# Softmax scores computed keys by queries instead of queries by keys, in a fused attention layer

## The chip, the cores and the metric

One core of one Trainium2 chip runs the whole layer. The metric is device time in microseconds (us) of one execution, the median over runs. Engines are named as the profile names them: PE is TensorE (PEld its weight loads), DVE VectorE, ACT ScalarE, POOL GpSimd, SP the engine that issues most DMAs.

## The reference, cut to what matters

A layer over 1024 tokens of width 1024: an input projection, a gated linear attention group (GLA, 4 heads, 16 chunks of 64), a softmax attention group (MLA, 8 heads, key width 96, value width 64), an output projection with residual, and a squared-ReLU MLP. The change touches the softmax attention:

```python
def one_block(args):                      # a block of 128 queries
    q_blk, blk = args
    s = jnp.einsum('bhqd,bhkd->bhqk', q_blk, kh, preferred_element_type=jnp.float32) * scale
    q_chunk = (blk * QBLOCK + jnp.arange(QBLOCK)) // CHUNK
    mask = key_chunk[None, :] <= q_chunk[:, None]         # CHUNK = 64
    p = jax.nn.softmax(jnp.where(mask, s, -1e30), axis=-1)
    return jnp.einsum('bhqk,bhkv->bhqv', p.astype(vh.dtype), vh)
```

Everything is float32. The projections and the MLP split each operand into a rounded part (type `fp32r`, names ending in `_hi`) and a remainder (`_lo`) and add three products. The softmax attention and the GLA products run in plain f32.

## The kernel before, in words

The program is written engine by engine; each engine walks its own fixed list of instructions, and semaphores tie the lists together. Stages follow each other: input projection (32 tiles, `in_project`, with the preparation of queries, keys and values behind it), attention, output projection (16 tiles, `project`), MLP up and MLP down.

The attention loop has 64 steps, one for each head and block of 128 queries (`STEPS`), two heads interleaved; 16 steps make a pair of heads, and there are four pairs. One step is this chain:

- PE `scores` (called two steps ahead): queries are the weights, keys are streamed, the result is 128 queries by up to 1024 keys in PSUM (banks 0 to 3).
- DVE `row_max` (L1627, L1630) writes the mask value into the corner that the block may not see and takes the negated maximum of each row.
- ACT `exp` (L1167) computes the exponential with that maximum as bias and adds up the row.
- DVE `row_sum` (L1634) takes the reciprocal of the sum, one column; POOL `normalize` (L907) multiplies the row by it.
- PE `p_transposes` (L2163) turns each 128x128 block, because the value product needs keys on the partitions; ACT and DVE `pT_copy` (L975, L1641) copy them out of PSUM banks 4 and 5.
- PE `values`: for two heads at once, each in its own 64 columns of the array, values are the weights and the turned exponentials are streamed, into bank 6.
- ACT `mla_mix_hi` and DVE `mla_mix_lo` split a finished unit (two heads by 512 queries) for the output projection.

Between these, every engine runs its share of GLA (`gla(c, n)`: chunk pair c in eight small stages n, all in PSUM bank 7). Stage 7 makes the output, ACT squares it (L1158), DVE sums the squares (L1587), POOL forms the reciprocal root (L796, L797), DVE scales the output (`og`, L1346), PE transposes it (L2083). In the loop before, stages 0 to 7 fall on consecutive steps.

The first two `scores` stand ahead of the last input projection tile (tile 31). The last transposes and values run inside the first two output projection tiles. PE's waits in `scores` are on ACT's exponentials two tiles back; SP loads queries, keys and GLA chunks one unit ahead (L570, L577, L584) and starts the pieces of the output weights (L549) at the start of the loop.

Of the kernel before, what the change touches and what calls it, by code (L numbers as in the profile page):

```python
# [12 lines left out]
P = 128  # L13
# [73 lines left out]
def layer(nc, x, positions, attn_norm, w_in, w_gate_up, b_gate, gla_out_norm, q_a_norm, w_uq,  # L87
# [9 lines left out]
    with ctx:  # L97
# [9 lines left out]
        def at(name, shape, offset, dt=F32):  # L107
# [56 lines left out]
        m_pT = at("m_pT", [P, 3, NB, P], 72 * KB)  # L164

        m_p = [at(f"m_p{n}", [P, T], offset * KB) for n, offset in enumerate((68, 88, 64))]
        m_v = at("m_v", [P, NB, MH * MV], 128 * KB)

        m_qT = [at(f"m_qT{n}", [DQK, 2, W], (144 + 4 * n) * KB) for n in range(2)]
        m_kT = [[at(f"m_kT{n}_{s}", [DQK, T], offset * KB) for s, offset in enumerate(places)]  # L170
                for n, places in enumerate(((152, 156), (84, 92)))]

        ke_tok = at("ke_tok", [P, GH * GDK], 168 * KB)
# [76 lines left out]
        m_nm = small("m_nm", [P, 2])  # L250
        m_sum = small("m_sum", [P, NB])
        m_rden = small("m_rden", [P, NB])
# [51 lines left out]
        q_in, k_in, z_in, v_in = ([sem(f"{name}{n}") for n in range(2)] for name in ("q_in", "k_in", "z_in", "v_in"))  # L304
        s_ready, max_ready, p_ready, rden_ready = sem("s_ready"), sem("max_ready"), sem("p_ready"), sem("rden_ready")
        pn_ready = sem("pn_ready")
        pT_ready, pT_out, pT_out2, pv_done = sem("pT_ready"), sem("pT_out"), sem("pT_out2"), sem("pv_done")
# [28 lines left out]

        def own_place(q, k):
            return q == 0 and k >= RING
# [16 lines left out]
        def low_by_vector(n):  # L355


            return KT <= n < KT * IN_GROUPS and n % KT in (2, 3, 4, 5)
# [142 lines left out]
        ORDER = (0, 3, 1, 2), (4, 7, 5, 6)  # L501
        STEPS = [(2 * p + s, b) for p in range(MH // 2) for half in range(2) for b in ORDER[half] for s in range(2)]
        UNIT = NB

        BEHIND = 3

        def half_of(i):
            return i // UNIT % 2

        def score_banks(i):  # L510

            return ((3, 2, 0, 1)[i % 4],) if half_of(i) == 0 else (2 * (i % 2), 2 * (i % 2) + 1)

        def scores_at(i):
            first, n = score_banks(i)[0], len(score_banks(i))
            return ps[:, first:first + n, :].rearrange("p a n -> p (a n)")

        def before_in_banks(i):

            return max((n for n in range(i) if set(score_banks(n)) & set(score_banks(i))), default=None)  # L520


        def by_scalar(i):
            return half_of(i) == 1 or i % 2 == 0

        def by_vector(i):
            return half_of(i) == 1 or i % 2 == 1

        def scalar_copies(i):

            return sum(by_scalar(n) for n in range(i + 1))

        def vector_copies(i):
            return sum(by_vector(n) for n in range(i + 1))

        def mix_due(i):

            j = (i - BEHIND) // 2
            if i >= BEHIND and (i - BEHIND) % 2 == 0 and j % 4 == 3:
                return j // 8, j // 4 % 2  # L540
            return None

        @block.sync
        def _(sp):
# [20 lines left out]
            def queries(u):  # L565

                if u >= 2:
                    sp.wait_ge(s_ready, UNIT * (u - 1))
                p, half = divmod(u, 2)
                sp.dma_start(m_qT[u % 2][:, :, :], q_d[2 * p:2 * p + 2, :, half * W:(half + 1) * W].rearrange("h d t -> d h t")  # L570
                             ).then_inc(q_in[u % 2], 16)

            def keys(p):
                if p >= 2:
                    sp.wait_ge(s_ready, 2 * UNIT * (p - 1))
                for s in range(2):
                    sp.dma_start(m_kT[p % 2][s][:, :], k_d[2 * p + s]).then_inc(k_in[p % 2], 16)  # L577
# [9 lines left out]
            def stores(s):  # L587
# [18 lines left out]
                if s == HEADS_T_AT[-1]:  # L606
                    sp.wait_ge(heads_stored, 32 * NB)
                    sp.wait_ge(v_stored, 16 * NB)
                    queries(0)
                    keys(0)  # L610
                    for n in range(2):
                        half = slice(n * NB // 2, (n + 1) * NB // 2)
                        sp.dma_start(m_v[:, half, :], v_d[half].rearrange("b p n -> p b n")).then_inc(v_in[n], 16)
                    queries(1)

            for q in range(IN_GROUPS):
# [10 lines left out]
                if q + 1 < IN_GROUPS:  # L627
                    for k in range(RING + 2, KT):
                        in_piece(q + 1, k)
                    if q == 0:  # L630
                        sp.dma_start(m_ukv[:, :], w_ukv[0]).then_inc(mla_w_in, 16)
                else:
                    for k in range(RING):
                        piece(IN_GROUPS, k, w_out_d[0, row_tile(IN_GROUPS, k)])
# [3 lines left out]
            for n in range(2):  # L638
                sp.wait_ge(z_stored[n], 16 * NB)
            for c in range(2):  # L640
                chunk_in(c)

            sp.wait_ge(z_ready, NB * IN_GROUPS)
            keys(1)
            for u in range(2, MH):
                if u % 2 == 0 and u >= 4:
                    keys(u // 2)
                queries(u)
                chunk_in(u)
# [3 lines left out]
            sp.wait_ge(pv_done, len(STEPS) // 2)  # L653
# [131 lines left out]
        def _(pool):  # L785
# [116 lines left out]
            def normalize(i):  # L902

                _, b = STEPS[i]
                rows = m_p[i % 3][:, 0:(b + 1) * P]
                pool.wait_ge(rden_ready, i + 1)
                pool.tensor_scalar(rows, rows, m_rden[:, i % NB:i % NB + 1], 1.0, ALU.mult, ALU.mult).then_inc(pn_ready, 1)  # L907

            for i in range(len(STEPS)):
                c, n = divmod(i, NB)  # L910
                normalize(i)
                if i == 0:
                    decays(0)
# [4 lines left out]
                if c == NB - 1 and n >= 1:  # L918
                    low_part(IN_GROUPS, n - 1)
            low_part(IN_GROUPS, KT - 1)  # L920
# [44 lines left out]
        def _(act):  # L965
# [194 lines left out]
            def exp(i):  # L1160
                h, b = STEPS[i]
                nk = (b + 1) * P
                act.wait_ge(max_ready, i + 1)
                if i >= 3:

                    act.wait_ge(pT_ready, 2 * (i - 2))
                act.activation(m_p[i % 3][:, 0:nk], scores_at(i)[:, 0:nk], ACT.Exp, bias=m_nm[:, i % 2:i % 2 + 1],  # L1167
                               accum_out=m_sum[:, i % NB:i % NB + 1]).then_inc(p_ready, 1)

            def pT_copy(i):  # L1170
                if by_scalar(i):
                    _, b = STEPS[i]
                    act.wait_ge(pT_ready, 2 * i + 1 + (half_of(i) == 0))
                    bank, n = (4, 4) if half_of(i) else (4 + i % 2, b + 1)
                    copy(m_pT[:, i % 3, 0:n, :], bank4(bank)[:, 0:n, :]).then_inc(pT_out, 1)
# [1153 lines left out]
```

## Time and profile before

| | us |
|---|---|
| median of 3 runs (1137.91 to 1140.94) | 1139.54 |
| the profiled execution: its own time | 1140.02 |
| the profiled execution: span from the first to the last instruction | 1138.0 |
| TensorE clock granted, mean over the span | 0.997 of full |

The page gives busy time per engine, then the chain of work that ended last, then groups of instructions. An engine that is busy 98% of the span is not at its peak, because the ends of pipelined matmuls are modelled: the distance between the starts of two matmuls says what one really takes. A plain f32 matmul leaves two records (two passes over its columns), an `fp32r` matmul and a transpose one. The attention stage runs from 237.4 us to 433.9 us of the span.

### The profile page before, as it was taken

What the parts mean: (1) busy time and instruction counts of PE and PEld (TensorE: products, weight loads), DVE (VectorE), ACT (ScalarE), POOL (GpSimd) and SP (SyncE); (2) the same over time, 40 slices, a digit from 0 to 9 for tenths busy, and PEclk for the clock granted to TensorE, in tenths of its full rate; (3) what the DMA queues carried; (4) which work ended last, traced back from release to release, by engine and by line L of the source; (5) the groups of instructions that cost most, each with busy time, mean ns of one, the idle gap of its engine ahead of it and who ended that gap; (6) DMA issues with size and microseconds to landing.
All of it is one profiled execution on the core that took longest, in us unless ns stands there. A gap on an engine that the chain in (4) does not pass through costs nothing.

```text
span 1138.0 us, 15337 instructions
## 1 busy us (share of the span) xinstructions
PE 1117.6 (98%) x5630; PEld 908.8 (80%) x5630; DVE 778.1 (68%) x1120; ACT 463.9 (41%) x876; POOL 511.2 (45%) x418
## 2 busy tenths in 40 slices
PE   7999999999999999999999999999999999999998
PEld 7978888776676678887888888888878888888887
DVE  5565767557777652278485875587797978888863
ACT  5343554336555552156223322332334334434341
POOL 2332513114433463147654444444545556565562
PEclk9999999999999999999999999999999999999999
DMA  7232523461221016213544333431789783457542
GB/s 253 67 130 74 167 84 112 116 194 33 61 74 47 26 38 240 74 75 111 161 137 142 116 112 130 139 121 37 261 277 359 234 290 121 139 180 232 197 119 86
DMA packets 98554, 158.41 MB, mean 139 GB/s; under 512 B 9329, under 2 KB 39041, under 8 KB 98481
## 3 DMA queue, kind: packets, MB, share of 16 engines
q1 hardware_dynamic: 96864, 152.80, 40.6%
q10 hardware_dynamic: 1296, 4.46, 1.1%
q8 instruction: 45, 0.74, 0.3%
q0 software_dynamic: 320, 0.19, 0.2%
q14 instruction: 29, 0.23, 0.1%
HBM read 115.47 MB, written 41.94 MB: 138 GB/s over the span
## 4 chain that ended last, share of the span: by engine, by line
PE 85%; DVE 7%; POOL 2%; ACT 2%; issue 2%; DMA 2%; SPq 0%; ACTq 0%; DVEq 0%; POOLq 0%
PE ps L1919 80%; PE ps L2163 2%; PE ps L2012 1%; DVE t_all L1691 1%; POOL tx_lo L932 1%; DVE dr_lo L1691 1%; DVE m_nm L1630 1%; DMA up_raw<-in_w_up_dram 1%; DMA raw<-in_w_in_dram 1%; PE ps L1934 1%; DMA m_ukv<-in_w_ukv_dram 1%; POOL ua_lo L937 1%; DVE state L1346 0%; DVE stage L1691 0%; POOL a_lo L932 0%
## 5 line engine op out<-in xcount | busy, mean ns | idle before, releaser
L1919 PE MATMUL ps<-dr_hi,dl_hi 128*128 128x512 f32 x448 | 175.1, 391 | 1.6 <-DVE dr_lo L1691 1.6
L1919 PE MATMUL ps<-dr_hi,dl_lo 128*128 128x512 f32 x448 | 175.0, 391 | 0.0
L1919 PE MATMUL ps<-dr_lo,dl_hi 128*128 128x512 f32 x448 | 174.9, 390 | 0.0
L937 POOL TENSOR_TENSOR ua_lo<-up_raw,ua_hi 128x1024 fp32r<-128x1024 f32 x46 | 116.7, 2541 | 117.0 <-ACT ua_hi L975 117.0
L961 POOL TENSOR_TENSOR dl_lo<-l_raw,dl_hi 128x512 fp32r<-128x512 f32 x64 | 100.3, 1593 | 72.7 <-ACT dl_hi L975 72.3
L961 POOL TENSOR_TENSOR dl_lo<-s_all,dl_hi 128x512 fp32r<-128x512 f32 x48 | 75.3, 1589 | 58.4 <-ACT dl_hi L975 57.6
L1919 PEld LDWEIGHTS ps<-dr_hi,dl_hi 128*128 128x128 f32 x448 | 84.5, 189 | 20.3 <-issue 2.8
L1919 PE MATMUL ps<-a_hi,ua_hi 128*128 128x512 f32 x256 | 99.9, 390 | 0.6 <-POOL ua_lo L937 0.6
L1919 PE MATMUL ps<-a_hi,ua_lo 128*128 128x512 f32 x256 | 99.6, 389 | 0.0
L1919 PE MATMUL ps<-a_lo,ua_hi 128*128 128x512 f32 x256 | 99.6, 389 | 0.0
L1919 PEld LDWEIGHTS ps<-dr_hi,dl_lo 128*128 128x128 f32 x448 | 84.4, 188 | 17.7
L1919 PEld LDWEIGHTS ps<-dr_lo,dl_hi 128*128 128x128 f32 x448 | 84.5, 189 | 17.4
L907 POOL TENSOR_SCALAR m_p<-m_p,m_rden 128x128 f32<-128x128 f32 (+7 forms) x64 | 52.9, 829 | 96.7 <-DVE m_rden L1634 96.2
L975 ACT ACTIVATE ua_hi<-up_raw 128x1024 fp32r<-128x1024 f32 x48 | 50.5, 1057 | 90.6 <-PE ps L1919 79.0
L1691 DVE TENSOR_TENSOR dr_lo<-r_raw,dr_hi 128x512 fp32r<-128x512 f32 x64 | 72.2, 1127 | 13.2 <-ACT dr_hi L975 13.1
L1919 PE MATMUL ps<-wi_hi,a_hi 128*128 128x512 f32 (+1 forms) x192 | 75.4, 393 | 2.8 <-DVE a_lo L1357 2.7
L1919 PE MATMUL ps<-m_kT,m_qT 96*128 96x512 f32 (+3 forms) x192 | 75.8, 505 | 1.2 <-ACT m_p L1167 1.2
L1691 DVE TENSOR_TENSOR dr_lo<-t_all,dr_hi 128x512 fp32r<-128x512 f32 x48 | 59.9, 1263 | 22.7 <-ACT dr_hi L975 22.3
L1919 PE MATMUL ps<-tx_hi,ua_hi 128*128 128x512 f32 x192 | 74.7, 389 | 0.0
L1919 PE MATMUL ps<-tx_lo,ua_hi 128*128 128x512 f32 x192 | 74.7, 389 | 0.0
L1919 PE MATMUL ps<-tx_hi,ua_lo 128*128 128x512 f32 x192 | 74.7, 389 | 0.0
L975 ACT ACTIVATE dl_hi<-l_raw 128x512 fp32r<-128x512 f32 x64 | 39.8, 622 | 85.1 <-PE ps L1919 79.3
(238 smaller groups left out, 2536.4 us busy)
## 6 DMA issues: line engine op xcount, KB each, us to landing
r_raw<-in_w_down_dram SPq DMA_DIRECT2D x144, 256.0 KB, 3.5
hidden<-stage SPq DMA_DIRECT2D x72, 256.0 KB, 2.0
up_raw<-in_w_up_dram SPq DMA_DIRECT2D x16, 1024.0 KB, 5.5
l_raw<-hidden SPq DMA_DIRECT2D x64, 256.0 KB, 3.6
raw<-in_w_in_dram SPq DMA_DIRECT2D x24, 256.0 KB, 3.5
z_gla<-z_stage SPq DMA_DIRECT2D x16, 256.0 KB, 2.0
raw<-in_w_out_dram SPq DMA_DIRECT2D x16, 256.0 KB, 6.4
xs<-in_x_dram SPq DMA_DIRECT2D x8, 512.0 KB, 7.6
```

The costliest lines, as they stand in the source:

```text
L907: pool.tensor_scalar(rows, rows, m_rden[:, i % NB:i % NB + 1], 1.0, ALU.mult, ALU.mult).then_inc(pn_ready, 1)
L932: pool.tensor_tensor(lo, t_new[n][:, :, :], hi.bitcast(F32), ALU.subtract).then_inc(tlo_done, 1)
L937: pool.tensor_tensor(ua_lo[n % UP_RING][:, :, :], up_source(g, product), ua_hi[n % UP_RING][:, :, :].bitcast(F32), ALU.subtract).then_inc( ...
L961: pool.tensor_tensor(slot(dl_lo, t), left_source(t), slot(dl_hi, t).bitcast(F32), ALU.subtract).then_inc(dllo_done, 1)
L975: return act.activation(dst, src, ACT.Copy, scale=scale)
L1630: dve.tensor_reduce(m_nm[:, i % 2:i % 2 + 1], s[:, 0:nk], AX.X, ALU.max, negate=True).then_inc(max_ready, 1)
L1691: return dve.tensor_tensor(out_, in0, in1, op)
L1919: return pe.matmul(dst, lhsT, rhs, start=start, stop=stop, skip_group_check=onto)
L1934: last = pe.transpose(bank4(4 + j)[:, i, :], src[:, (4 * j + i) * P:(4 * j + i + 1) * P], ident[:, :])
L2012: last = pe.transpose(bank4(4 + i // 4, DQK)[:, i % 4, :], m_qk[:, b % 2, i, :], ident[:, :])
L2163: last = pe.transpose(bank4(bank)[:, c % 4, :], m_p[i % 3][:, c * P:(c + 1) * P], ident[:, :])
```

## The change

It replaces the attention loop. Scores are computed with keys as the weights and queries streamed, so the exponentials come out with keys on the partitions, which is what the value product takes. The row maximum must then be known before the scores: a first pass (`estimate`) computes queries by keys from operands rounded to `fp32r`, DVE takes the maxima of that, PE turns the table of maxima once for a unit, and a DMA lays it as row 97 of the queries; a row of ones stands under the keys, so the score product subtracts the maximum itself. Sums over keys now run across partitions: POOL adds up the exponential tiles of a unit, and PE multiplies that by a matrix of ones (`sums`, bank 4). DVE then takes the reciprocal of 512 columns and multiplies the finished unit (`mla_divide`).

The loop has 24 steps of two tiles (a tile: 128 keys by up to 512 queries, two heads), six steps (S0, S1, L0 to L3) for a pair of heads: S steps belong to the first 512 queries (4 tiles), L steps to the second 512 (8 tiles). Each pair takes 12 estimates, 12 tiles, 2 turns, 2 sums. The places of GLA stages are given by a table. Input projection tiles 29 to 31 are interleaved with the first nine estimates. The first pieces of the output weights are loaded when the last pair begins.

```diff
+        STEPS = 6 * MH // 2
+        TILES = [(u, c) for u in range(UNITS) for c in range(NB // 2 * (u % 2 + 1))]
+        ESTIMATES = {(S0, 0): (1, 5), (S0, 1): (1, 6), (S0, 2): (1, 7), (L0, 2): (2, 0), (L0, 3): (2, 1), (L1, 1): (2, 2),
+                     (L1, 2): (2, 3), (L2, 0): (3, 0), (L2, 1): (3, 1), (L2, 2): (3, 2), (L2, 3): (3, 3), (L3, 1): (3, 4)}
+        GLA_AT = ((-1, 0, 1, 2), (None, 3, None, None), (4, None, 5, 6), (7, 8, 9, 10), (11, 12, None, 13),
+                  (None, 14, None, None))
...
+            def maxima(u):
+                sp.wait_ge(turned_out, u + 1)
+                sp.dma_start(m_q[queries_at(u)][DQK:DQK + 1, :, :].rearrange("o s (b n) -> o (s b) n", n=P),
+                             m_row[:, u % 2, :]).then_inc(q_in[u % 3], 16)
...
-            def normalize(i):
...
-                pool.tensor_scalar(rows, rows, m_rden[:, i % NB:i % NB + 1], 1.0, ALU.mult, ALU.mult).then_inc(pn_ready, 1)
...
+            def add(j):
...
+                pool.tensor_tensor(total, total, p_tile(j)[:, :, seen], ALU.add).then_inc(sum_done, 1)
...
+            def round_queries(u):
...
+                copy(m_q_hi[n][:, :, :], m_q[n][0:DQK, :, :]).then_inc(mla_hi, 1)
+            def round_keys(p):
...
+                copy(m_k_hi[keys_hi_at(p)][:, :, :], m_k[p % 2][0:DQK, :, :]).then_inc(mla_hi, 1)
...
+            def exp(j):
...
+                to, scores = p_tile(j), ps[:, score_bank(j):score_bank(j) + 2, :]
+                first = first_query(j)
+                if diagonal(j):
+                    own = slice(first, first + CHUNK)
+                    act.activation(to[CHUNK:P, :, own], ident[CHUNK:P, :].rearrange("p (s n) -> p s n", s=2), ACT.Copy, scale=0.0)
+                    act.activation(to[0:CHUNK, :, own], scores[0:CHUNK, :, own], ACT.Exp)
+                    first += CHUNK
+                act.activation(to[:, :, first:W], scores[:, :, first:W], ACT.Exp).then_inc(p_ready, 1)
...
+            def mla_divide(u):
+                dve.wait_ge(den_ready, u + 1)
+                dve.wait_ge(raw_out, u + 1)
+                step(dve.reciprocal(ps[:, 4, :], ps[:, 4, :]))
+                dve.tensor_tensor(m_raw[u][:, :], m_raw[u][:, :], ps[:, 4, :], ALU.mult).then_inc(raw_ready, 1)
...
+            def estimate(e):
...
+                    pe.wait_ge(max_ready, e)
+                if sums_before(e):
+                    pe.wait_ge(raw_ready, sums_before(e))
...
+            def sums(u, estimates):
+                pe.wait_ge(max_ready, estimates)
+                if u >= 1:
+                    pe.wait_ge(raw_ready, u)
+                pe.wait_ge(sum_done, in_ring(first_of(u + 1)))
+                for s in range(2):
+                    last = mm(ps[s * MV:(s + 1) * MV, 4, :], ones[:, 0:MV], p_first[u % 2][:, s, :], True, True)
...
+            def scores(j):
...
+                for s in range(2):
+                    last = mm(ps[:, score_bank(j) + s, seen], m_k[p % 2][:, s, c * P:(c + 1) * P],
+                              m_q[queries_at(u)][:, s, seen], True, True)
...
+            for d in range(STEPS):
+                between_scores(d, 0)
+                if d >= 1:
+                    scores(2 * d)
+                linear(d, 0)
+                between_scores(d, 1)
+                scores(2 * d + 1)
+                linear(d, 1)
+                between_scores(d, 2)
+                if d >= 1:
+                    values(d - 1)
+                linear(d, 2)
+                between_scores(d, 3)
+                linear(d, 3)
+                between_scores(d, 4)
```

## Rows read from the trace of the kernel before

**Rows 1.** The page: busy time of the engines, and the chain by engine.
```profile
PE 1117.6 (98%) x5630; PEld 908.8 (80%) x5630; DVE 778.1 (68%) x1120; ACT 463.9 (41%) x876; POOL 511.2 (45%) x418
...
PE 85%; DVE 7%; POOL 2%; ACT 2%; issue 2%; DMA 2%; SPq 0%; ACTq 0%; DVEq 0%; POOLq 0%
```

**Rows 2.** One pair's stretch: length, busy PE, PEld, DVE, ACT, POOL, clock, DMA.
```profile
291.40:336.80 45.40, 43.85 (x334) 31.30 (x333) 33.01 (x94) 25.56 (x63) 18.61 (x24) 1.00 0.20 59
```

**Rows 3.** Timeline: start, length; f32 scores, transposes, values, `fp32r` products.
```profile
297.33 0.38 PE L2163 MATMUL ps<-ident,m_p 128*128 128x128 f32 x2
...
297.64 1.09 PE L1919 MATMUL ps<-m_pT,m_v 128*64 128x128 f32 x16
...
299.64 0.19 PEld L1919 LDWEIGHTS ps<-m_kT,m_qT 96*128 96x128 f32 x1 [0.24 <-issue]
300.07 0.19 PEld L1919 LDWEIGHTS ps<-m_kT,m_qT 96*128 96x128 f32 x1 [0.24 <-issue]
...
314.24 1.06 PE L2163 MATMUL ps<-ident,m_p 128*128 128x128 f32 x8
...
315.24 1.31 PE L1919 MATMUL ps<-m_pT,m_v 128*64 128x128 f32 x20
...
422.05 0.39 PE L1919 MATMUL ps<-w_hi,a_hi 128*128 128x512 f32 x1
...
424.76 0.39 PE L1919 MATMUL ps<-w_hi,a_hi 128*128 128x512 f32 x1
```

**Rows 4.** Groups of 291.4 to 336.8 us: PE, with count, busy us, mean ns, idle.
```profile
L1919 PE MATMUL ps<-m_kT,m_qT 96*128 96x512 f32 x24 | 12.5, 614 | 0.3 <-ACT m_p L1167 0.3
L2163 PE MATMUL ps<-ident,m_p 128*128 128x128 f32 x73 | 10.9, 274 | 0.7 <-DVE m_pT L1641 0.7
```

**Rows 5.** The same stretch, DVE: reductions, GLA work, reciprocal, two-input product.
```profile
L1346 DVE SCALAR_TENSOR_TENSOR state<-state,decay,ps 64x128 f32<-64x128 f32 x8 | 2.8, 346 | 0.9 <-PE ps L1919 0.8
L1634 DVE RECIPROCAL m_rden<-m_sum 128x1 f32<-128x1 f32 x16 | 2.5, 156 | 1.2 <-ACT m_p L1167 1.2
L1630 DVE TENSOR_REDUCE m_nm<-ps 128x1 f32<-128x1024 f32 x2 | 2.4, 1224 | 0.1
L1346 DVE SCALAR_TENSOR_TENSOR og<-ps,g_rs,zg 128x128 f32<-128x128 f32 x8 | 2.2, 338 | 0.0
L1587 DVE TENSOR_REDUCE g_ss<-osq 128x4 f32<-128x512 f32 x2 | 1.4, 676 | 1.0 <-ACT osq L1158 1.0
L1555 DVE TENSOR_TENSOR g_ks<-g_ks,zqkT 128x256 f32<-128x256 f32 x2 | 0.8, 410 | 0.0
```

**Rows 6.** The page and the stretch of rows 4: POOL and ACT.
```profile
L937 POOL TENSOR_TENSOR ua_lo<-up_raw,ua_hi 128x1024 fp32r<-128x1024 f32 x46 | 116.7, 2541 | 117.0 <-ACT ua_hi L975 117.0
L975 ACT ACTIVATE ua_hi<-up_raw 128x1024 fp32r<-128x1024 f32 x48 | 50.5, 1057 | 90.6 <-PE ps L1919 79.0
L797 POOL TENSOR_TENSOR g_rs<-g_rs,minus_half 128x4 f32<-128x4 f32 x2 | 2.0, 1014 | 0.2
L1167 ACT ACTIVATE m_p<-ps,m_nm 128x1024 f32<-128x1024 f32 x2 | 2.2, 1114 | 1.9 <-DVE m_nm L1630 1.9
```

**Rows 7.** DVE elsewhere: a product of 512 columns (52 to 66 us), a scan.
```profile
L1503 DVE TENSOR_TENSOR wi_lo<-raw,wi_hi 128x512 fp32r<-128x512 f32 x4 | 2.5, 685 | 0.0
...
L1446 DVE TENSOR_TENSOR_SCAN g_cum<-ones,g_cum 128x128 f32<-128x128 f32 x16 | 5.3, 401 | 0.1
```

**Rows 8.** Timeline at the start of attention: key loads and DVE's scan.
```profile
221.39 1.00 SPq L577 DMA_DIRECT2D m_kT<-k_heads  x2
...
228.32 2.63 DVE L1446 TENSOR_TENSOR_SCAN g_cum<-ones,g_cum 128x128 f32<-128x128 f32 x8
```

**Rows 9.** Key tiles, 214 to 240 us: from issue to landing.
```profile
DMA to landing us min/median/max: 5.4/5.7/5.9
```

**Rows 10.** Timeline at the end of attention: first projection product, last values.
```profile
421.27 0.48 PE L1919 MATMUL ps<-w_hi,a_hi 128*128 128x512 f32 x1
...
431.79 1.75 PE L1919 MATMUL ps<-m_pT,m_v 128*64 128x128 f32 x28
```

More of the change, by code:

```diff
@@ L495, in layer @@
         GATE_T, SOFTPLUS, GATE_SUMS = NB, 3 * NB, 3 * NB + 3
[L501 to L540, printed above, removed]
-            return None
+        UNITS = MH
@@ L1655, in _ @@
+            for s in range(NB * IN_GROUPS - 4, NB * IN_GROUPS - 1):
+                tile_out(s)
+                behind(s)
+                if s == NB * IN_GROUPS - 3:
+                    for e in (2, 3, 4):
+                        row_max(e)
+                    gla_decays(0)
+                elif s < NB * IN_GROUPS - 3:
+                    for e in (0, 1):
+                        row_max(e)
+            for e in (5, 6):
+                row_max(e)
             gla_decayed(0)
+            for e in (7, 8):
+                row_max(e)
@@ L1954, in in_project @@
                 for k in range(KT):
-                    if between is not None and k == KT - 2:
-                        between()
+                    if k in between:
+                        between[k]()
                     if n in LOGIT_TILES and k == 3:
@@ new lines, in values @@
+            def values(d):
+                for j in (2 * d, 2 * d + 1):
+                    u, c = TILES[j]
+                    pe.wait_ge(p_ready, j + 1)
+                    if j == 0:
+                        pe.wait_ge(v_in, 16 * MH // 2)
+                    if c == 0 and u >= 1:
+                        pe.wait_ge(raw_out, u)
+                    seen = slice(first_query(j), W)
+                    for s in range(2):
+                        last = mm(ps[s * MV:(s + 1) * MV, 6, seen], m_v[:, u // 2, c, s * MV:(s + 1) * MV],
+                                  p_tile(j)[:, s, seen], c == 0, j + 1 == first_of(u + 1), True)
+                    last.then_inc(pv_done, 1)
@@ new lines, in between_scores, with linear @@
+            def between_scores(d, place):
+                if estimate_at(d, place) is not None:
+                    estimate(estimate_at(d, place))
+                if turned_at(d, place) is not None:
+                    turn(turned_at(d, place))
+                u = sums_at(d, place)
+                if u is not None:
+                    sums(u, min(first_of(u + 2) + 2 if u % 2 == 0 else first_of(u + 3), len(TILES)))
+            def linear(d, place):
+                if gla_at(d, place):
+                    gla(*gla_at(d, place))
@@ new lines, in _ @@
+            for n in range(NB * IN_GROUPS - 3, NB * IN_GROUPS):
+                in_project(*divmod(n, NB), {
+                    NB * IN_GROUPS - 3: {4: lambda: estimate(0), 6: lambda: estimate(1)},
+                    NB * IN_GROUPS - 2: {0: lambda: estimate(2), 2: lambda: estimate(3), 4: lambda: turn(0), 6: lambda: estimate(4)},
+                    NB * IN_GROUPS - 1: {0: lambda: estimate(5), 2: lambda: estimate(6), 3: lambda: scores(0),
+                                         4: lambda: estimate(7), 6: lambda: estimate(8)}}[n])
```

520 lines of the change are left out of this document (313 added, 207 removed).

## The prediction

> **What bounds the kernel now.** The page comes first. PE is busy 98% of the span and carries 85% of the chain that ended last, so the time is the sum of what PE issues and of what it waits for; other engines count only where PE stands behind them [rows 1]. The stretches show the attention loop repeating with a period of 45.4 us, one pair of heads each (four in all, three of them alike), at a granted clock of 1.00, the upper level (2.4 GHz). DVE is busy for 33.0 us of a period, ACT for 25.6, POOL for 18.6 [rows 2]. The timeline gives what a matmul really takes. Two passes of an f32 score start 0.43 us apart for 512 columns. Eight transposes last 1.06 us with a tail of 0.27, so one takes (1.06 - 0.27)/7 = 0.113. Twenty value records take (1.31 - 0.27)/19 = 0.055 each for 128 columns, half of what scores take per column, because two heads run side by side. Twelve `fp32r` products of 512 columns take 2.71, 0.226 each. A change of group costs about 0.1: two transposes (0.23) are followed by values after 0.31 [rows 3].
>
> Work of a period: scores 9216 columns, 15.4 us; 72 transposes, 8.1; values 7.9; GLA, whose 68 records go by the same rates, 7.1. Sum 38.5. What is left to 45.4, 6.9 us, is some 50 changes of group (5) and waits; the groups name 1.0 of these, on the copies of turned exponentials (0.7) and on ACT (0.3) [rows 4].
>
> **The change, part by part, for one pair of heads.**
>
> Transposes go: -8.1 us. Scores and values keep their columns: 0. The copies of turned exponentials and POOL's normalization were hidden under PE save for the waits named above; they are worth no more than those.
>
> Estimates come: 12 of them, 9472 columns at 0.226 for 512: +4.2. Sums: two units of four passes of 512 columns. If the two halves run side by side as values do, a unit costs 2 x 0.43 = 0.86, if not 1.72 [rows 3]; I take 1.1, nearer the row of values, as the form is the same: +2.2. Two turns: +0.2. PE's work becomes 37.0, 1.5 less. Changes of group: 12 scores, 12 estimates, 12 tiles of values of which half need a wait of their own, 2 turns, 2 sums, 12 of GLA, about 45, 4.5 us. PE alone would need 41.5 against 45.4.
>
> The new waits decide. I walked one period, engine by engine, in the order of the lists.
>
> S0: PE issues estimate, scores, the GLA output, estimate, scores, estimate, short values, and stands before the transposes of `og` after 7.3 us. The output ended at 4.1. Behind it DVE takes a row maximum (1.22, with the mask's corner 1.4), the sum of squares (0.68), POOL the root (1.01 and a short one), DVE a second row maximum in its shadow and `og` (four of 0.34 that overlap, 1.1): 9.3 [rows 5, 6]. Wait: 1.9. Before, these stages lay on consecutive steps of 2.8 us, now on places some 1.5 us apart.
>
> Behind the transposes in PE's list stand the turn and the next step's scores, so ACT's exponentials start later by as much. L0: `sums` wait for the row maximum of the second estimate, which on DVE is queued behind the GLA state (four of 0.35): 1.5. L1: `og` again, 1.4. S1, L2 and L3 show none above 0.2. Together 4.8, and a period of 41.5 + 4.8 = 46.3, 0.9 more than before.
>
> The division. DVE takes a reciprocal of 512 columns twice a pair, where it took 16 of one column. No row shows a wide one. The lower bound is one column per step like the two-input product, 0.14 + 512 x 1.07 ns = 0.69. DVE's scan takes (401 - 135)/128 = 2.1 ns per column [rows 7], so operations do differ; this would give 1.2. The one-column reciprocal takes 156 ns where the line through the products of 256 columns (410) and of 512 (685) leaves 136 for one column [rows 5, 7]: 20 ns for a single column, which read as the price of a column would be 10 us for 512, the upper bound. Part of these 20 may be start-up. I take eight steps per column, 8 x 512 x 1.07 ns + 0.14 = 4.5 us, between the two and nearer the row of the same instruction.
>
> The Trainium skill (page VectorE: DVE Perf Modes, section First, the fixed hardware budget) says that reciprocal runs on iterative divide operations "with a repeat count of 8". With the rate of an ordinary pass the sum would be the first rival's below, with eight steps it is mine.
>
> At 4.5 us the division is 3.8 longer than an ordinary pass. In L0 and L1: the sums end at 24.0 in the period, the division at 29.2; PE comes to the estimate that needs bank 4 free at 27.5, and waits 1.7. In S1 the odd unit's division ends 3.8 later; ACT's list has the split of that unit (which needs it) ahead of rounding queries (1.06) and keys (2 x 1.06) and of the next exponential [rows 6]; the copy of a GLA tile behind these comes 1.0 late for PE. Together 2.7 per pair; the first pair has no odd unit before it and the last no estimates after it: 1.6 + 2.7 + 2.7 + 1.0 = 8.0.
>
> Hidden, and what if not: exponentials, 28 instructions a pair instead of 16 with no sum read out, some 15 us of 46 on ACT (1024 columns 1.11) [rows 6]; if late, `scores` wait two tiles on. POOL's adds, 7168 columns a pair at 2.54 for 1024: 17.8 [rows 6], in place of the normalizations; behind a ring of four tiles; if late, `sums` come first. The DMA of the maxima: turned at the end of S0, needed a step later, about 2.5 us against 4.8. On SP's list it stands behind loads of keys, queries and chunks, and these wait only for things done earlier.
>
> **Start.** Keys are issued at 221.4 and land 5.7 later, at 227.1 [rows 8, 9]; ACT rounds keys (2.1) and queries (1.06): 230.2. The first estimate stands at 229.3 in tile 29: 0.9 of waiting. DVE is held by its scan until 231.0 [rows 8], which delays the second one little. The nine estimates and the first scores are work that the loop has less of. The turns wait for row maxima of 1.22: 1.6. Start: +2.5. The first pair has no `og` in S0: -1.9.
>
> **End.** Before, projection starts at 421.27, with the last transposes and values (1.75) left inside its first two tiles [rows 10]. After, only sums and `og` are left. The output weights are loaded later, and their fourth to seventh piece hang on remainders made in the last two steps; I count 0 for it, and up to 3 if a piece is late.
>
> **Sum** against the profiled execution's own 1140.0 (span 1138.0 and 2.0 around it): 4 x 0.9 - 1.9 + 2.5 + 8.0 = +12.2; the last pair also drops 1.5 of waits of L0, where no estimates stand: +10.7. That is 1150.7, and 0.5 less on the scale of the median 1139.5: 1150. A difference under 0.3%, 3.4 us, can't be told from none.
>
> **Rivals.**
>
> First: the wide reciprocal runs like any pass. Then the 8.0 go: 1142, within 0.3%. For it: nearly all DVE rows lie on one line. Against: the 20 ns. It takes the place of the forecast if the group of wide reciprocals shows under 1.5. Range 1138 to 1147. Chance 0.2.
>
> Second, the faster end: PE stays the bound, because the chains on DVE are shorter than I walked them. DVE loses 12 copies of 3840 columns (3840 x 1.07 ns + 12 x 0.14 = 5.8 a period) and the small reciprocals (2.5) and gains 2 x 1.4; its load falls from 33 to some 27.5 of 45 [rows 2, 5]. If every wait above is covered, a pair takes 41.5, and 4 x 3.9 = 15.6 are saved, less 2.5 at the start: 1127. With half of the waits left, 1136. It decides from the point where `og` reaches PE within 3.2 us of the GLA output. Against: that chain has 1.37 + 0.68 + 1.2 + 1.1 us in it. Chance 0.25.
>
> Third: DVE becomes the bound. With 4.5 for a division, DVE has 27 + 7.6 = 35 us of work in 46; if a division near the upper bound (10 us) is true, every step falls behind and a pair takes about 6 us more than in my forecast: 1170. Chance 0.08.
>
> Fourth: the change doesn't remove what it says, for instance values of 512 columns no longer run side by side. Then values cost 7.9 more a pair: 1180. Against: the rows of values and of the GLA form both overlap in narrow columns. Chance 0.02.
>
> My forecast keeps 0.45, with a range of its own of 1144 to 1158.
>
> **How the numbers follow.** Faster by over 0.3% (under 1136): the second rival, 0.25. Within: most of the first and the edge of the forecast, 0.17. Slower: 0.58. The range leaves out the third and fourth rival above and the lower half of the second below: 1130 to 1161.
>
> **What would show each step.** In the changed profile: the group of RECIPROCAL 128x512 at 4.5 us, not 0.7; PE idle before the transposes of `og` released by DVE, 1.4 to 1.9 us, seven times; PE idle before estimates released by DVE's product into `m_raw`; busy time by period 46 to 49 us instead of 45.4. Wrong it would be if the period is under 44 us, if PE's idle time sits on ACT or POOL instead of DVE, or if the first scores of a unit wait for the DMA of the maxima.

## The result, and the profile after

The changed kernel takes 1198.86 us (median of 4 runs, 1198.18 to 1199.98), the kernel before 1138.93 beside it: a ratio of 1.0525, 95% interval 1.0507 to 1.0543. That is 60 us slower. The forecast was 1150, 11 us slower, with a range that ended at 1161: right in sign, wrong in size by more than the range allowed. All ratios here are of undisturbed executions; one of the kernel before, 1323 us at a mean clock of 0.794, is left out beside the fifth plan.

The page of the changed kernel: its span, busy times, the slices of PE and of the granted clock, and the chain by engine.

```profile
span 1198.2 us, 14071 instructions
...
PE 1151.5 (96%) x5094; PEld 891.6 (74%) x5094; DVE 796.5 (66%) x996; ACT 466.8 (39%) x842; POOL 523.7 (44%) x390
...
PE   8999999987979798999999999999999999999998
...
PEclk9999999987878787999999999999999999999999
...
PE 84%; DVE 9%; issue 2%; POOL 2%; DMA 2%; ACT 1%; SPq 0%; DVEq 0%; ACTq 0%; POOLq 0%
```

PE's busy time went up from 1117.6 to 1151.5 us though it issues 536 matmuls fewer [rows 1]. Work of fewer columns that takes longer is the sign of a lower clock, and the row PEclk shows it: 8 and 7 in the attention (slices 9 to 16), and nowhere else. Now the same in stretches; the columns are those of [rows 2], the clock third from the end.

```profile
319.30:380.70 61.40, 52.63 (x200) 27.43 (x200) 37.25 (x62) 24.82 (x54) 22.93 (x18) 0.81 0.16 43
...
244.00:480.00 236.00, 203.69 (x750) 105.78 (x750) 136.68 (x225) 95.93 (x202) 90.60 (x70) 0.80 0.14 40
```

A pair of heads takes 61.4 us; it took 45.4 [rows 2]. From the first scores to the first product of the output projection the attention takes 240.1 us (244.1 to 484.2) in place of 183.6, so 56.5 us of the loss are in it; the first scores stand 6.4 later, and some 3 come back behind. The clock in the attention stood at 1.00 before and at 0.80 now. Inside a pair it has two levels:

```profile
283.00:287.00 4.00, 0.86 (x5) 0.43 (x5) 3.23 (x5) 0.29 (x2) 3.86 (x2) 1.00 0.00 0
287.00:304.00 17.00, 15.34 (x33) 7.46 (x34) 4.52 (x9) 4.44 (x9) 6.90 (x4) 0.50 0.10 32
304.00:317.00 13.00, 11.97 (x62) 7.23 (x61) 10.39 (x20) 6.97 (x19) 3.23 (x5) 0.99 0.38 91
```

For 4 us (283 to 287) PE is busy for 0.86. Then comes a stretch of 17 us in which PE is busy 90% of the time and the granted clock is 0.50, the lower of its two levels (1.2 GHz); PE does 33 matmuls in it, against 62 in the next 13 us. This repeats in each of the first three pairs; in the fourth the clock stays at 0.50 for some 14 us. What does PE wait for? The waits of PE in the pair from 319.3 us (in total, times, longest):

```profile
PE ps L2281 <- DVE og L1523: 4.8, 2, 3.1
PE ps L2114 <- DVE m_nm L1804: 2.0, 1, 2.0
PE ps L2114 <- ACT m_q_hi L1083: 1.7, 1, 1.7
PE ps L2114 <- DVE m_nm L1809: 0.2, 1, 0.2
```

Together 8.7 us, of which four waits make 8.5: 1.7 before `og`'s transposes in S0, 2.0 before the sums at the end of L0, 3.1 before `og`'s transposes in L1 and, right behind these, 1.7 before the first estimate of L2. The timeline of L1 shows how the two come together (DVE, then PE, then POOL, then ACT):

```profile
340.75 0.96 DVE L1804 TENSOR_REDUCE m_nm<-ps 128x2 f32<-128x768 f32 x1
341.62 0.68 DVE L1764 TENSOR_REDUCE g_ss<-osq 128x4 f32<-128x512 f32 x1
342.73 0.17 DVE L1803 MEMSET ps<- 64x128 f32 x1 [0.43 <-PE ps L2114]
342.93 1.23 DVE L1804 TENSOR_REDUCE m_nm<-ps 128x2 f32<-128x1024 f32 x1
344.07 2.62 DVE L1819 TENSOR_TENSOR a_lo<-m_raw,a_hi 128x512 fp32r<-128x512 f32 x1
346.62 1.11 DVE L1523 SCALAR_TENSOR_TENSOR og<-ps,g_rs,zg 128x128 f32<-128x128 f32 x4
```

```profile
344.44 0.27 PE L2354 MATMUL ps<-ident,m_nm 128*8 128x128 f32 x1
347.79 0.66 PE L2281 MATMUL ps<-ident,og 128*128 128x128 f32 x4 [3.08 <-DVE og L1523]
350.16 0.87 PE L2114 MATMUL ps<-m_k_hi,m_q_hi 96*128 96x320 f32 x2 [1.72 <-ACT m_q_hi L1083]
```

```profile
343.80 7.59 POOL L1009 TENSOR_TENSOR p_first<-p_first,p_ring 128x1024 f32<-128x1024 f32 x3
```

```profile
348.48 0.60 ACT L1083 ACTIVATE a_hi<-ps 128x512 fp32r<-128x512 f32 x1 [3.46 <-PE ps L2281]
348.97 1.04 ACT L1083 ACTIVATE m_q_hi<-m_q 96x1024 fp32r<-96x1024 f32 x1
```

DVE's list has `mla_mix_lo` (L1819) ahead of `og`. A product of 512 columns took 0.685 us before [rows 7]; this one takes 2.62, while POOL adds. `og` ends at 347.7, PE transposes, and ACT, whose list has the copy of the transposed tile ahead of the rounding of the queries, gives PE its next estimate only at 350.0. So it goes in the first three pairs. In the fourth no adds stand beside the lower part, which takes 0.68 us (at 462.0), and `og` waits for POOL's root instead; PE waits the same 3.1.

And the division, the largest unknown of the forecast, with the lower part of the MLA tile (groups of DVE, 240 to 430 us):

```profile
L1814 DVE RECIPROCAL ps<-ps 128x512 f32<-128x512 f32 x5 | 16.8, 3367 | 2.8 <-PE ps L2114 2.8
L1819 DVE TENSOR_TENSOR a_lo<-m_raw,a_hi 128x512 fp32r<-128x512 f32 x5 | 9.7, 1936 | 0.7 <-ACT a_hi L1083 0.7
```

3.37 us, where I had taken 4.5. So the clock, the waits and the division stand beside each other as possible causes. The theory (A): the waits make up some 9 us a pair, and what is more, they make the clock fall, which costs as much again. The rivals: (B) the new mixture of products lowers the clock, whatever the waits; (C) the clock is a bystander and the waits are the loss; (D) the division holds up the chains.

### The profile page after: what moved, and what is told of

Same layout as the page of the kernel before. It is cut to its first block, busy times and chain, and to the rows that moved or that the text cites. A ratio compares the mean times of both kernels' runs of the same rounds, so it can differ in the third digit from the quotient of the medians.

```text
span 1198.2 us, 14071 instructions
## 1 busy us (share of the span) xinstructions
PE 1151.5 (96%) x5094; PEld 891.6 (74%) x5094; DVE 796.5 (66%) x996; ACT 466.8 (39%) x842; POOL 523.7 (44%) x390
## 4 chain that ended last, share of the span: by engine, by line
PE 84%; DVE 9%; issue 2%; POOL 2%; DMA 2%; ACT 1%; SPq 0%; DVEq 0%; ACTq 0%; POOLq 0%
PE ps L2114 81%; PE ps L2210 1%; DVE t_all L1886 1%; POOL tx_lo L1040 1%; DVE m_nm L1809 1%; DVE a_lo L1819 1%; DVE dr_lo L1886 1%; DVE og L1523 1%; DMA up_raw<-in_w_up_dram 1%; PE ps L2281 1%; DMA raw<-in_w_in_dram 1%; PE ps L2129 1%; POOL ua_lo L1045 0%; DMA m_ukv<-in_w_ukv_dram 0%; DVE stage L1886 0%
## 5 line engine op out<-in xcount | busy, mean ns | idle before, releaser
L2114 PEld LDWEIGHTS ps<-dr_hi,dl_lo 128*128 128x128 f32 x448 | 84.1, 188 | 17.4
L1009 POOL TENSOR_TENSOR p_first<-p_first,p_ring 128x1024 f32<-128x1024 f32 (+3 forms) x40 | 69.9, 1747 | 60.3 <-PE ps L2114 35.0
L2114 PE MATMUL ps<-m_q,m_k 97*128 97x512 f32 (+3 forms) x192 | 89.4, 600 | 0.0
L2114 PE MATMUL ps<-wi_hi,a_lo 128*128 128x512 f32 (+1 forms) x192 | 73.5, 383 | 0.0
```

The lines of the kernel that those rows point to most:

```text
L1009: pool.tensor_tensor(total, total, p_tile(j)[:, :, seen], ALU.add).then_inc(sum_done, 1)
L2114: return pe.matmul(dst, lhsT, rhs, start=start, stop=stop, skip_group_check=onto)
```

## The experiments

**Filling the waits.** Products whose results nobody reads, in front of the four waits (the lines that call `fill` are left out; in the diffs that follow, too, only the lines that carry the change are shown):

```diff
+ def fill(d, n):
+     pe.wait_ge(p_ready, 2 * d + 1)
+     for i in range(n):
+         mm(ps[:, 2, 0:P], ident[:, :], ident[:, :], True, True)
+ FILL = {(S0, 3, "gla"): 8, (L1, 3, "gla"): 13, (L2, 0, "est"): 8, (L0, 4, "est"): 9}
```

> Adds matrix products of the identity with itself (128 columns, f32, about 0.23 us each at the full clock, results never read) on TensorE ahead of the four waits: 8 before the output transposes in the first step of a pair, 9 before the sums in the third, 13 before the output transposes in the fourth, 8 before the estimate that opens the fifth; they fill about 9 us of each pair's 61.4. Theory A (the clock falls because TensorE stands idle in these waits, and that is most of the loss): the granted clock of the attention is back at 1.00, the pair takes 51 to 53 us, the kernel 1155 to 1168 us. Rival B (the clock falls because of the new mixture of products, whatever the waits): the clock stays near 0.80, the time 1198 or more. Rival C (the waits themselves are the loss and the clock a bystander): 1198.

Measured: 1169.98 us, ratio 1.0272 (1.0254 to 1.0289), 29 us faster than the changed kernel, with nothing taken from it and 152 products added. A pair of it:

```profile
326.40:378.40 52.00, 50.89 (x274) 31.93 (x274) 37.15 (x63) 24.84 (x53) 22.96 (x18) 1.00 0.19 52
```

52.0 us at a clock of 1.00. B falls, since all of the new mixture is in it; C falls, since PE can start its useful work no sooner than before: the products that fill the four places take 9.2 us of the pair, the waits there took 8.5. DVE, ACT and POOL do the same work in the pair (37.2, 24.8, 23.0 us) as without the filling. The 60 us split in two. By the profiled spans, 1198.2 - 1164.7 = 33.5 us are the clock, and 1164.7 - 1138.0 = 26.7 (4 x 6.6 by the pairs) the waits less PE's savings; by the medians, 29 and 30, since the profiled execution of the filled kernel was its fastest (mean clock 0.999, the three others 0.994). The clock's part is rather more than that, because the filling is not free: 0.7 us more a pair than the waits, and a new wait of 0.6 for the division's product. The Trainium skill (TensorE: Matmul & The Clock Gate, Part 1: The HAM clock gate) says that a monitor gates this clock by how busy TensorE has recently been; this run agrees, with 1.00 in a pair where the four places are busy and 0.81 where they are idle.

**Filling only the fourth step's waits** (`{(L1, 3, "gla"): 13, (L2, 0, "est"): 8}`).

> Only the two waits around the output transposes of the fourth step are filled with products of the identity (13 and 8); those of the first step (1.7) and before the sums (2.0) stay. In the changed kernel the granted clock stands at half level for 17 us behind the fourth step's waits and for 3.4 us twice elsewhere in a pair. Theory A: the 17 us stretches go, the 3.4 us ones stay: the time lies nearer to the kernel with all four filled (1170) than to the changed kernel (1199): 1172 to 1182. Rival (every idle stretch counts alike, by its length): half of the gain stays out, 1183 to 1190.

Measured: 1175.45, ratio 1.0319 (1.0302 to 1.0335). 23 of the 29 us come from these two waits (4.8 of 8.7 us); the other two, 1.7 and 2.0 us long and far from each other, give 6. If idle time counted by its length alone, 4.8 of 8.5 us would give 16. It is the two waits next to each other, PE busy 0.86 of 4 us, that cost most.

**The same wait in the kernel before.** This has none of the change; the first lines are DVE's, in `gla_out`:

```diff
+ for _ in range(5):
+     step(dve.tensor_tensor(osq[:, :, :].rearrange("p a n -> p (a n)"), zg[:, c % 2, :], zg[:, c % 2, :], ALU.max))
  for h in range(GH):
      last = stt(og[:, h, :], ...
```

> The kernel before, with five passes of 512 columns on VectorE (some 0.7 us each, results never read) ahead of each of the eight outputs of the linear attention, so that TensorE has to wait for the output before it transposes it. Nothing of the softmax change is in it. Theory A: TensorE waits 1 to 3 us in 7 places, the granted clock of the attention falls below 1.00 as in the changed kernel, and the time rises by more than the waits add up to. Rival B (the fall of the clock belongs to the new products): the clock stays at 1.00 and the time rises by the waits alone. If VectorE's queue has over 3 us of room there: the same time as before.

Measured: 1196.52, ratio 1.0494 (1.0458 to 1.0529), 58 us slower. Its slices of the clock, a pair of it, and PE's waits in the attention:

```profile
PEclk9999999998787878999999999999999999999999
```

```profile
330.50:392.00 61.50, 52.64 (x332) 37.12 (x332) 41.86 (x105) 25.75 (x63) 19.35 (x25) 0.83 0.15 44
```

```profile
PE ps L2085 <- DVE og L1346: 29.7, 7, 6.4
```

The old kernel with one late operation takes 61.5 us a pair, at a clock of 0.83. Seven waits of 29.7 us in all cost 58. That is theory A in a kernel without a single estimate, sum or division. The waits are longer than was meant (1 to 3 us expected, 4.2 in the mean, up to 6.4) and longer than those of the changed kernel, so this shows that waits bring the clock down whatever the products, not how little waiting is enough.

**The output's transposes one step later.** In `GLA_AT`:

```diff
- ((-1, 0, 1, 2), (None, 3, None, None), (4, None, 5, 6), (7, 8, 9, 10), (11, 12, None, 13),
-  (None, 14, None, None))
+ ((-1, 0, 1, None), (None, 2, None, 3), (4, None, 5, 6), (7, 8, 9, None), (10, 11, 12, 13),
+  (None, 14, None, None))
```

> One table is changed: the transposes of the linear attention's output, their rounding and lower parts come one step later (first step's to the second step, fourth step's to the start of the fifth). Theory A: two of the four waits of TensorE (1.9 and 3.1 us) go, 5 us of a pair or 20 in all, and part of the clock comes back with them: 1150 to 1175 us. Rival B (clock independent of the waits): 1178 us, with the clock still near 0.80. If the chain behind the output is only moved (the masks and scores of the next chunk then wait in its place): over 1190.

Measured: 1178.15, ratio 1.0340 (1.0313 to 1.0366); 20.7 us gained. The time is outside what A gave (up to 1175) and is the 1178 of rival B. But B wanted the clock near 0.80, and in a pair of 54.0 us it is 0.94, so B is out by the clock, not by the time. The two waits for `og` are gone, and others came out from under them (waits of PE, 324 to 378 us):

```profile
PE ps L2114 <- DVE m_nm L1804: 2.0, 1, 2.0
PE ps L2114 <- DVE a_lo L1778: 1.8, 2, 1.3
PE ps L2114 <- POOL p_first L1009: 1.6, 1, 1.6
PE ps L2114 <- ACT m_q_hi L1083: 1.4, 1, 1.4
PE ps L2354 <- DVE m_nm L1809: 0.7, 1, 0.7
PE ps L2114 <- ACT ke_tok L1083: 0.5, 1, 0.5
PE ps L2114 <- DVE m_nm L1809: 0.4, 2, 0.2
```

Together they are 8.4 us in nine places, the longest 2.0, where the changed kernel had 8.7 in five, the longest 3.1. PE waits as long as before, and a pair is 7.4 us shorter. So nearly all of this gain is the clock's, and how the waits are spread counts beside their sum. This speaks against C without any filling.

**No reciprocal.** DVE writes a constant in 0.70 us in place of the reciprocal in 3.37; the exponentials' products stay undivided.

```diff
- step(dve.reciprocal(ps[:, 4, :], ps[:, 4, :]))
+ step(dve.tensor_scalar(ps[:, 4, :], ps[:, 4, :], 0.0, 0.01, ALU.mult, ALU.add))
```

> Leaves out the reciprocal of the 128 x 512 sums: VectorE writes a constant there in its place (an op of about 0.7 us for one of 3.37), the multiply stays; 2.7 us less of VectorE per unit, 5.3 per pair. Theory A: TensorE's four waits do not begin behind the reciprocal in the trace, so the time falls by 1 us per pair at most: 1192 to 1199. Rival D (the division is what holds VectorE back, and so the chains that TensorE waits for): the waits shorten by the 2.7 us each time, the clock follows, 1150 to 1180.

Measured: 1196.59, ratio 1.0507 (1.0491 to 1.0522): 2.3 us. PE's waits in the pair from 319.3 us are those of the changed kernel to a tenth of a microsecond (4.8, 2.0, 1.7, 0.2). D falls for these pairs; only in the last pair does the wait for `og` change, from 3.1 to 1.1 us.

**No adds either.** GpSimd adds 8 columns of each tile, so the sums are left out as well:

```diff
- pool.tensor_tensor(total, total, p_tile(j)[:, :, seen], ALU.add)
+ pool.tensor_tensor(total[:, :, 0:8], total[:, :, 0:8], p_tile(j)[:, :, seen][:, :, 0:8], ALU.add)
```

> As the kernel without the reciprocal, and GpSimd adds 8 columns of each tile in place of all (the sums are left out). Theory A with the shared access: VectorE's lower part of the MLA tile falls from about 1.6 to 2.6 us to 0.7, the output of the fourth step comes 1.9 us sooner, 8 us in all and some of the clock: 10 to 25 us under the kernel without the reciprocal. Rival (GpSimd's adds slow nothing on VectorE): the same time as that kernel, and the lower part still over 1.5 us.

Measured: 1179.17, ratio 1.0352 (1.0335 to 1.0369), 17.4 us under the kernel without the reciprocal. The lower part's group and that of its sister without the reciprocal, then the lower part without the adds as well, and PE's wait for `og` in that last kernel (240 to 430 us; the wait, 319.3 to 380.7):

```profile
L1819 DVE TENSOR_TENSOR a_lo<-m_raw,a_hi 128x512 fp32r<-128x512 f32 x5 | 12.2, 2434 | 1.8 <-ACT a_hi L1083 1.8
...
L1778 DVE TENSOR_TENSOR a_lo<-ps,a_hi 128x512 fp32r<-128x512 f32 x5 | 3.5, 690 | 7.8 <-ACT a_hi L1083 7.8
```

```profile
L1819 DVE TENSOR_TENSOR a_lo<-m_raw,a_hi 128x512 fp32r<-128x512 f32 x5 | 3.4, 685 | 1.8 <-ACT a_hi L1083 1.8
```

```profile
PE ps L2281 <- DVE og L1523: 2.9, 2, 1.7
```

2434 ns beside the adds, 685 without them. Its sister L1778, the same product with one input in PSUM, takes 690 beside the adds. So GpSimd's adds hold up a DVE product with two inputs in SBUF. In L1, where the product takes 2.62 us with the adds, the wait for `og` falls by the same 1.9 us, from 4.8 to 2.9 a pair. The Trainium skill (SBUF — State Buffer, section Who interferes with whom) says that a DVE instruction with two SBUF inputs contends with a GpSimd instruction that reads SBUF; these rows agree, with 2434 against 685 ns. Of the 17 us, 5.8 are shorter waits for `og` (15.5 to 9.7 in the whole attention) and 2.8 a wait for the last exponentials that the kernel without the reciprocal has and this one has not; the rest goes with the clock, whose mean over the profiled executions rose from 0.966 to 0.973, but was not measured apart. The place where it counts, L1, is the same with and without the reciprocal: the lower part starts behind the row maximum (5 us after the division's end in the changed kernel), takes 2.62 us beside the adds, and `og` comes after it. That is why taking the reciprocal out did not help.

**Plans without the waits.** If A is right, the same work in another order should bring the time back. First plan: `og` as above, and

```diff
- ESTIMATES = {(S0, 0): (1, 5), (S0, 1): (1, 6), (S0, 2): (1, 7), (L0, 2): (2, 0), (L0, 3): (2, 1), (L1, 1): (2, 2),
-              (L1, 2): (2, 3), (L2, 0): (3, 0), (L2, 1): (3, 1), (L2, 2): (3, 2), (L2, 3): (3, 3), (L3, 1): (3, 4)}
+ ESTIMATES = {(S0, 1): (1, 5), (S0, 2): (1, 6), (S0, 3): (1, 7), (L0, 1): (2, 0), (L0, 3): (2, 1), (L1, 1): (2, 2),
+              (L1, 2): (2, 3), (L2, 1): (3, 0), (L2, 2): (3, 1), (L2, 3): (3, 2), (L3, 1): (3, 3), (L3, 2): (3, 4)}
  turned_at: S0 4 -> S1 1, L1 3 -> L2 0;  sums_at: L0 4 -> L3 3, S1 0 -> S1 1
```

The odd unit's division is done in two halves, and the splits of the MLA tiles come later. The work is the same.

> A new plan of the steps for the changed kernel, the same work: the linear attention's output transposes one step later; estimates from the second to the last place of the steps; the sums of a unit of even number at the end of the pair (division in the next first step), those of the odd one at the second place of the second step, with its division in two halves around the mask; maxima turned a step later; lower parts of the MLA tiles later still. Theory A: the four waits (8.6 us of a pair) shrink to under 3, the clock is back at 0.98 or more in the attention, a pair takes 44 to 47 us, the kernel 1138 to 1155. Rival B: the clock stays near 0.80 in the attention: over 1165.

Measured: 1161.94, ratio 1.0204 (1.0181 to 1.0227), 51.1 us a pair at a clock of 0.97: above the range that A gave, because seven waits of 0.5 to 1.5 us were left. It is also below the 1165 that B gave as the least. The reciprocal of a half, 256 columns, took 1758 ns.

Second plan:

```diff
  GLA_AT = ((-1, 0, None, 1), (None, 2, None, 3), (4, None, 5, 6), (7, 8, None, 9), (10, None, 11, 12), (13, 14, None, None))
  ESTIMATES: (2, 0) at L0 2; (3, 0) to (3, 4) at L2 2, L2 3, L3 0, L3 1, L3 3;  sums_at: L3 3 -> L1 3
```

The even unit's division stands behind the output in L1, and the splits of the MLA tiles are moved with it.

> A second plan of the steps, the same work: against the first plan, the sums of the even unit at the end of the fourth step with its division behind the output, the estimates of the odd unit from the third place of the fifth step on, the first estimate of the next even unit one place later, the masks and states of the second chunk a place or two later, the output of the first step a place later. In the first plan TensorE still waited 6.4 us of a pair of 51.1 in seven places (0.5 to 1.5 each) and the granted clock was 0.97 in the attention. Theory A: the waits shrink to some 2 us, the clock to 0.99 or more, a pair takes 46 to 48 us, the kernel 1142 to 1152. Rival: the waits move to other places (VectorE is the bound of the pair by then): 1158 to 1165.

Measured: 1144.46 (9 runs, 1142.47 to 1152.31), ratio 1.0041 (1.0029 to 1.0054). The profiled execution was the one of 1152.31; a pair of it, and a stretch behind the first pair's waits of 1.5 and 0.65 us (252 to 257.5 us):

```profile
307.70:352.40 44.70, 42.15 (x198) 22.89 (x198) 35.20 (x67) 24.98 (x54) 22.83 (x19) 1.00 0.22 60
256.00:280.00 24.00, 23.36 (x78) 12.64 (x76) 7.33 (x18) 12.36 (x21) 5.03 (x5) 0.64 0.06 18
```

A pair is now shorter than before the change. The stretch from 256 us is the likely difference between 1152 and the other runs (1142 to 1146): their mean clocks are on record too, 0.994 to 0.996 against 0.985. Where their clocks fell is not known.

Third plan:

```diff
  estimate_at, first two steps: 9 at S0 0, 10 at S0 2, 11 at S1 1
  ESTIMATES: (2, 0), (2, 1), (2, 2), (2, 3) at L0 1, L0 2, L0 3, L1 1;  turned_at: S1 1 -> S1 2
  sums_at: S1 1 -> S1 2, L1 3 -> L1 2;  the division of L1 in two halves, `og` between them
```

> A third plan, the same work: in the second plan a pair took 44.7 us with 2.35 of waits, and in the first pair the waits of 1.5 and 0.65 us brought the granted clock down for some 25 us in the profiled execution. Now the estimates of the first pair stand apart, the estimates of the even unit come from the second place of the third step on, its sums one place earlier, and the maxima of the odd unit are turned one place later. Theory A: the waits fall to some 1 us of a pair, the clock is 1.00 throughout, a pair takes 43.5 to 44.5 us, the kernel 1133 to 1142 and its runs lie closer together than those of the second plan (1142 to 1152). Rival: the maxima's row lands too late for the first scores of the third step, or the waits only move: 1143 to 1150.

Measured: 1145.34, ratio 1.0061 (1.0042 to 1.0079): a miss for A, which gave 1133 to 1142, inside the rival's 1143 to 1150 and level with the second plan. A pair took 44.5 us. The even unit's division is hidden, but `og` in S1 now comes 1.2 us late, behind the row maxima.

Fourth plan:

```diff
  ESTIMATES: (1, 7) at S1 1 instead of S0 3
  last group of the input projection: estimates 8 and 9 at k = 5 and 7;  first two steps: 10 at S0 0, 11 at S0 2
```

> The third plan with three moves: the last estimate of the odd unit at the second place of the second step (TensorE waited 0.7 us ahead of it in the step before, and 1.2 us for the output behind its row maxima on VectorE), and in front of the attention two more of the first pair's estimates between the products of the last group, so that the first pair has no waits of 0.6 and 1.1 us. In the third plan a pair took 44.5 us with 2.3 of waits. Theory A: a pair takes 42.5 to 43.5 us, the clock stays at 1.00 from the start, and the kernel takes 1133 to 1139 us, level with the kernel before or under it, its runs within 3 us of each other. Rival: the wait turns up at the turn of the maxima or behind their transfer, and the time stays at 1142 or more.

Measured: 1139.45 (11 runs, 1137.49 to 1141.58), ratio 1.0007 (0.9998 to 1.0016): no difference from the kernel before, and at the upper edge of what A gave (1133 to 1139). A pair takes 43.1 us.

Fifth plan:

```diff
  GpSimd, step STEPS - 2: out_low_parts(range(3)) ahead of the two adds instead of behind them
- for k in ((0, 1, 2), (3, 4, 5), (6,))[d - STEPS + 3]:
+ for k in ((0, 1, 2), (3, 4), (5, 6))[d - STEPS + 3]:
```

> The fourth plan with its end mended: there TensorE waits 2.0 and 0.8 us ahead of the last values, because ScalarE rounds the output projection's fifth slice of weights before the last exponentials, and that slice's transfer waits for a ring place that GpSimd frees only behind three adds; the granted clock then falls for one stretch. Now GpSimd makes the lower parts of the first slices ahead of the adds of that step, and ScalarE takes two slices in each of the last two steps in place of three and one. Theory A: both waits and the fall behind them go: 3 to 4 us under the fourth plan's 1139.4, so 1135 to 1137 us and faster than the kernel before by 0.2 to 0.4%. Rival: the adds come later by the 3 us of the lower parts, the last exponentials and sums with them, and the time stays at 1138 to 1141.

Measured: 1134.62 (11 runs, 1132.77 to 1136.83), ratio 0.9969 (0.9960 to 0.9978). All of the softmax change is in it, and it is faster than the kernel before by 0.3%. The stretch of a pair, PE's waits in it, and the page's two rows:

```profile
297.60:340.60 43.00, 41.53 (x199) 23.16 (x198) 35.30 (x67) 24.94 (x53) 22.74 (x19) 1.00 0.23 62
```

```profile
PE ps L2364 <- DVE m_nm L1811: 0.7, 1, 0.7
PE ps L2124 <- DVE m_raw L1819: 0.3, 1, 0.3
PE ps L2124 <- DVE m_nm L1806: 0.2, 1, 0.2
```

```profile
PE   8999999999999999999999999999999999999998
...
PEclk9999999999999999999999999999999999999999
```

The waits are 1.2 us of 43.0, and DVE, at 35.3, is not the bound.

## Why the prediction was wrong, step by step

- **The step that failed is one that the prediction did not take**: it read the granted clock of 1.00 in [rows 2] and carried it into a kernel in which PE would wait more. "41.5 + 4.8 = 46.3" adds waits to work at a fixed speed. The filled kernel shows that the waits also slow the work behind them: at least 33.5 of the 60.2 us between the profiled spans. The clock of 1.00 held in a kernel that hardly waits (98% in [rows 1]); at 8.7 us of waits a pair it was 0.80. The second failure is the size of these waits, 8.7 us a pair for 4.8. With it alone, at a fixed clock, the time would have been near that of the filled kernel (1170), outside the range too.
- **PE alone, 41.5 us**: right. The fifth plan's pair less its waits is 43.0 - 1.2 = 41.8. The sums do run side by side, as was taken. The other terms were not measured apart.
- **The wait in S0, 1.9**: 1.7, by the chain that was walked. **The wait in L0, 1.5**: 2.0. **The wait in L1, 1.4**: 3.1, in the first three pairs because the list of DVE was followed but the lower part of the MLA tile, which stands ahead of `og` in it, was priced as a product on its own (0.685). Beside GpSimd's adds it took 2.62. POOL's adds were called hidden, and their price was put at nothing.
- **"Others below 0.2"**: wrong by the 1.7 before L2's first estimate. ACT rounds the queries behind the copy that waits for `og`'s transposes; the prediction called ACT's work hidden by its busy time, and did not ask what is queued behind a wait.
- **The division, 4.5 us and 8.0 in all**: 3.37 us, and 2.3 in all when taken away. In steps of an ordinary pass (1.07 ns) it takes 5.9 a column, not the eight that were taken; the measured 6.3 ns decides. The wait of 1.7 behind it in L1 did not exist, since the late `og` came first. The place in the list mattered more than the price.
- **Start, +2.5**: the first scores stand at 244.1 us in place of 237.7. Ahead of them are now seven of the nine estimates (4864 columns, 2.1 us at the rate of [rows 3]), nine products of the last projection tile (2.0), which stood behind them before, and waits of 1.0 where 0.9 + 1.6 were forecast; the rest is changes of group. Two waits that the forecast lacks, 1.4 and 1.5 us for row maxima, stand in the first pair at 251 to 258 us. They were only moved, in the third and fourth plans, together with other edits. **End, up to 3**: in the fourth plan there were 2.8 us of it, and the piece named (the fourth to the seventh) was the one.
- **The rivals**: the second, that PE stays bound (1127 to 1136), is what the fifth plan reaches, 1134.6; its condition, `og` within PE's reach, needed another order of the steps. The third, DVE as the bound (1170), was nearest to the result by its number and had nothing to do with it: DVE was busy for 37.3 of 61.4 us.
- **The tests**: the seven waits for `og` came (1.7 us three times and 3.1 four times, 1.4 to 1.9 forecast), the division's sign did not, and "a period of 46 to 49" was broken by 61.4. Idle time on ACT, which the prediction named as what would prove it wrong, is there.

## What to carry to other kernels

In this kernel the granted clock of 1.00 held only while TensorE hardly waited. For a change that adds waits to such a kernel, look for places where they stand close together, and price the work behind them at the lower level as the unfavourable end of the range. When the clock falls in a trace, filling the waits with products nobody reads splits the loss into waiting and speed. Walk each engine's list past every wait, and price a vector product with two SBUF inputs by whether GpSimd adds beside it.

## What was not expected of the hardware

- The granted clock stood at 0.50 for 17 us behind 4 us in which TensorE was busy for 0.86, and did so three times in one kernel, though TensorE was busy for 15.3 of the 17. In the kernel with only the fourth step's waits filled, waits of 1.7 and 2.0 us stay and the mean clock of the whole run is 0.990. How long the clock stays down differs for the same place: behind the waits of 1.4 and 1.5 us in the first pair it was two stretches of 3.4 us in the changed kernel and one of 13.7 in this one. In the fifth plan, with no wait over 0.7 us in the pair shown, it is 0.998, and 1.00 in that pair.
- A reciprocal on VectorE took 3367 ns for 512 columns and 1758 for 256: 6.3 ns per column and 149 ns once. The 156 ns for one column [rows 5] lie on the same line, so the 20 ns that the prediction saw in it were not the price of a column.
- A VectorE product of 512 columns with both inputs in SBUF took 685 ns alone; with GpSimd's adds (2.4 us each for 1024 columns) in the kernel it took 1936 in the mean, 2434 without the reciprocal, and 2.63 us at the most seen. With one input in PSUM it took 690 beside them.
